# Attention probabilities of 43 steps and 16 tiles of a norm: transposed by DMA instead of by TensorE and the PSUM moves

## The chip, the cores and the metric

The kernel runs on the 8 cores of one Trainium2 chip. Each core works on one batch element of [2048, 1024] (the same program, other data); the cores don't speak to one another. The time is device microseconds (us) of the slowest core, from runs of the whole program. Engines are named as in the profile: PE is TensorE (matmuls and transposes), DVE VectorE, ACT ScalarE, POOL GpSimd, SP SyncE, which here only issues DMA.

## The reference, cut to what matters

Two layers. Layer 0 mixes tokens by dilated attention (three groups of heads with windows and dilations (128, 1), (512, 4), (2048, 16)) beside a convolution module; layer 1 by a short gated convolution. Every layer then adds and normalises, runs a SwiGLU FFN, normalises again and adds a gated embedding of p.

```python
# one head group; queries in blocks of 128, keys of the previous and of the own block
sc = jnp.einsum("brnqhe,brnkhe->brnhqk", qb, kk) * (e ** -0.5)
sc = jnp.where(mask[None, None, :, None], sc, NEG_INF)
m = jnp.max(sc, axis=-1, keepdims=True)
ex = jnp.exp(sc - m)
den = jnp.sum(ex, axis=-1)
o = jnp.einsum("brnhqk,brnkhe->brnqhe", ex, vv) / jnp.moveaxis(den, -1, -2)[..., None]
lse = m[..., 0] + jnp.log(den)
...
attn = sum over groups of softmax(lse over groups) * o
conv = silu(layer_norm(causal_depthwise_conv(a * sigmoid(gate), conv_w) + conv_b))
x = layer_norm(alpha * x + concat([attn, conv]) @ w_out)     # layer 0; layer 1: short_conv_mixer
x = layer_norm(alpha * x + swiglu(x))
x = x + (p[i] @ w_p) * sigmoid(x @ w_g)
```

## The kernel before, in words

Activations are held twice: as tokens (x_tok, 16 tiles of 128 tokens by 1024) and transposed (xT, 8 slabs of 128 channels by 2048 tokens), because every matmul contracts over partitions. Weights stream in by DMA on POOL's queue.

**Layer 0's mixer** works on 6 units (head group, pair of heads; UNITS). The even_order() list, written out by hand (L58 on), gives one order of events, and each engine walks the list and does its part of each event. In stage n (n = 0 to 5) unit n is projected, in 8 turns i: "qk" events with q/k matmuls (L559) and V matmuls (L586); VectorE applies the rotary embedding (L1191 to L1200), POOL adds the halves (rope_add, L1625). Between stages 0 and 1 lies the *gated stage*: 16 gated projections of the convolution module (L663), with attention steps 0 to 7 woven in. In stages 2 to 5 the attention of the unit projected before is woven in, step a = 8(n-1)+i at turn i, and stage 5 does unit 4 and unit 5, two steps in a pair of turns. An attention step (48 of them) handles two blocks of 128 queries of two heads:

- "s" scores(a): 8 matmuls (L602) into PSUM; VectorE masks (L1215) and takes the minimum (L1221) of the negated scores.
- "e" exponentials(a): ScalarE, four activations (L937) into Pb[a % 2].
- "t" transpose_p(a): PE transposes Pb in 4 to 8 tiles of 128x128 (L618) into PTB[0], a PSUM bank that it shares with "z", "cb" (conv_back, L697) and "mb" (merged_back, L648). The users of the bank follow one another in the order BANK0, and each waits until the one before it has been read (read0). p_move(a) copies the bank to PTt[a % 2], on ScalarE (L947) for the 32 steps of P_ON_ACT, on VectorE (L1233) for the other 16.
- "o" outputs(a): 4 to 8 matmuls of PTt with Vb (L636) into PTB[1]; ScalarE copies it to Ust (u_move, L968), and SP stores it to the scratch tensor scr (store_u, L1811).

"s" of a step comes at turn i, "e" at the start of the next turn, "t" in that turn behind the projections and "o" in the turn behind it (in the gated stage and in stage 5 further behind). Between "e" and "o" of one step lies about one turn in stages 2 to 4. In stages 2 to 4 "cb" and "cp" put the convolution's result back; in stages 4 and 5 the merge of the three groups runs ("ll" load_rows of scr into La, "ms", "mg", "mb"; L1827 to L1845, L987, L1280), with weights from statistics that go by scratch memory: ACT stores scs (L960), SP loads STL (load_statistics, L1815), VectorE computes them ("mw", L1245 to L1262).

**DMA queues.** SP, in the order of the list: scr stores, statistics, load_rows, x tiles (load_x), parameters, and in layer 1 and at both layers' ends DMA transposes of 128x1024 bf16 tiles (back1 L1870, back2 L1881, back3 L1888). POOL: load_unit(n+1) at the start of stage n (L1597, three times 512 KB), Wt, base, WmixE (L1679, 2 MB, stage 4, turn 2), later the FFN's ring pieces (L1588) and Wfo (L1693, 1 MB).

**Mixer output and the first norm of layer 0**: "out" mixer_out(t) for 16 tiles (L714), VectorE adds and normalises, ScalarE casts the tile to castt[t % 2]; norm_back(t) transposes it on PE (transpose_tile, L533) into PTB[1], three tiles behind, and ScalarE copies it to xT (L1097). The last tiles' events stand in ORDER[0], the FFN's list. FFN: L812 in, L838 out.

Of the kernel before, what the change touches and what calls it, by code (L numbers as in the profile page):

```python
# [6 lines left out]
BF16 = mybir.dt.bfloat16  # L7
# [5 lines left out]
NT = 16  # L13
# [6 lines left out]
K = 1024  # L20
# [19 lines left out]
WARM = 24  # L40
P_ON_ACT = [*range(8, 16), *range(24, 48)]

# [143 lines left out]
def build():  # L186
# [109 lines left out]
    dlt32 = sb("dlt32", [128, 8], F32, off_dg0)  # L296
    Pb = sb2("Pb", [128, 4, 256], BF16, off_dg0, 2 * K)
    sS = [sb("sS0", [128, 4, 256], F32, off_dg0 + 4 * K), sb("sS1", [128, 4, 256], F32, off_dg1 + 4 * K)]
# [26 lines left out]
    def half(i):  # L325
# [15 lines left out]

    pe_s, dve_ms, dve_mn, act_exp, pe_t, dve_pt, act_pt = (sem(n) for n in (
        "pe_s", "dve_ms", "dve_mn", "act_exp", "pe_t", "dve_pt", "act_pt"))
    pe_u, act_u = sem("pe_u"), sem("act_u")
# [16 lines left out]
    dve_xg1, dve_aff1 = sem("dve_xg1"), sem("dve_aff1")  # L361
    act_cast1, pe_tr1, act_xT1, d_x1 = sem("act_cast1"), sem("pe_tr1"), sem("act_xT1"), [sem("d_x1%d" % i) for i in range(2)]

# [121 lines left out]

    BANK0 = [u for u in EVEN if u[0] in ("t", "z", "cb", "mb")]
    BEFORE = dict(zip(BANK0[1:], BANK0))
# [42 lines left out]
    def tensor_program(pe):  # L530
# [77 lines left out]
        def transpose_p(a):  # L608
            if a == 0:
                pe.wait_ge(dve_const, 1)  # L610
# [4 lines left out]
            for bi, blk in enumerate(step_blocks(a)):  # L615
                for h in range(2):
                    for c in range(2 if qblock(UNITS[a // 8][1], blk)[0] else 1):
                        mm = pe.transpose(out=PTB[0][:, n * 128:(n + 1) * 128],  # L618
                                          in_=Pb[a % 2][:, 2 * bi + h, c * 128:(c + 1) * 128], identity=ident[:])
                        n += 1  # L620
            mm.then_inc(pe_t, 1)

# [44 lines left out]
        def phases_to_rows(c):  # L667
            if c == 0:
                pe.wait_ge(dve_glu, 16)
            pe.wait_ge(*read0(("z", c)))  # L670
# [46 lines left out]

        def norm_back(t):
            pe.wait_ge(act_cast1, t + 1)
            if t >= 1:  # L720
                pe.wait_ge(act_xT1, t)
            else:
                pe.wait_ge(act_u, 48)
            transpose_tile(castt[t % 2], 1, 8).then_inc(pe_tr1, 1)

        def even_mixer():
            for kind, v in EVEN:
                if kind == "qk":
                    project(*v)
                elif kind == "v7":  # L730
                    last_v()
                elif kind == "glu":
                    gated(v)
                elif kind == "s":
                    scores(v)
                elif kind == "t":
                    transpose_p(v)
                elif kind == "o":
                    outputs(v)
                elif kind == "z":  # L740
                    phases_to_rows(v)
                elif kind == "cv":
                    convolve(v)
                elif kind == "cb":
                    conv_back(v)
                elif kind == "mb":
                    merged_back(v)
                elif kind == "out":
                    mixer_out(v)
                elif kind == "nm" and v >= 3:  # L750
                    norm_back(v - 3)

# [16 lines left out]
        def layer_tail(l):  # L769
# [4 lines left out]
            for kind, a, b in ORDER[l]:  # L774
# [8 lines left out]
                if kind == "mo":  # L783
# [8 lines left out]
                    mm.then_inc(pe_mo, 1)  # L792
                elif kind == "tr1":
                    t = a
                    if l == 0:
                        norm_back(t)
# [99 lines left out]
        for i in range(WARM):  # L896
            pe.matmul(PD[2][:, 0:512], lhsT=Pb[1][:, 0, 0:128], rhs=Pb[1][:, 0:2, :].rearrange("p a b -> p (a b)"),
                      start=True, stop=True)
# [6 lines left out]
    def scalar_program(act):  # L905
# [22 lines left out]
        def exponentials(a):  # L928
            act.wait_ge(dve_mn, a + 1)
            if a >= 2:  # L930
                act.wait_ge(pe_t, a - 1)
            for i in range(4):
                bi, h = divmod(i, 2)
                blk = step_blocks(a)[bi]
                nk = 256 if qblock(UNITS[a // 8][1], blk)[0] else 128
                sblk = st_block(UNITS[a // 8][1], blk)
                act.activation(out=Pb[a % 2][:, i, 0:nk], in_=sS[a % 2][:, 2 * h + bi, 0:nk], func=AF.Exp, scale=-1.0,  # L937
                               bias=ST[:, a // 8, sblk, 2 + h:3 + h],
                               accum_out=ST[:, a // 8, sblk, h:h + 1]).then_inc(act_exp, 1)

        def p_move(a):
            if a not in P_ON_ACT:
                return
            n = 128 * sum(4 if qblock(UNITS[a // 8][1], b)[0] else 2 for b in step_blocks(a))
            act.wait_ge(pe_t, a + 1)
            act.wait_ge(pe_u, a - 1)
            act.activation(out=PTt[a % 2][:, 0:n], in_=PTB[0][:, 0:n], func=AF.Copy).then_inc(act_pt, 1)  # L947
# [74 lines left out]
        def even_mixer():  # L1022
# [6 lines left out]
            for kind, v in EVEN:  # L1029
# [19 lines left out]
                elif kind == "e":  # L1049
                    exponentials(v)  # L1050
                elif kind == "t":
                    p_move(v)
# [29 lines left out]
        def norm_slot(l, s):  # L1082
            t = s - 2
            if 0 <= t < NT:
                n = 16 * l + t
                act.wait_ge(dve_aff1, n + 1)
                if t >= 2 and l == 0:
                    act.wait_ge(pe_tr1, t - 1)
                elif t >= 2:
                    act.wait_ge(d_x1[t % 2], 16 * (t // 2))  # L1090
                act.activation(out=castt[t % 2][:], in_=x_tok[:, t, :], func=AF.Copy).then_inc(act_cast1, 1)
            if s < NT:
                squares(l, s)
            t = s - 3
# [91 lines left out]
    def vector_program(dve):  # L1186
# [16 lines left out]
        def masked(a):  # L1203
# [20 lines left out]
            d.then_inc(dve_mn, 1)  # L1224

        def p_move(a):
            if a in P_ON_ACT:
                return
            n = 128 * sum(4 if qblock(UNITS[a // 8][1], b)[0] else 2 for b in step_blocks(a))
            dve.wait_ge(pe_t, a + 1)  # L1230
            if a >= 2:
                dve.wait_ge(pe_u, a - 1)
            dve.tensor_copy(out=PTt[a % 2][:, 0:n], in_=PTB[0][:, 0:n]).then_inc(dve_pt, 1)  # L1233

# [104 lines left out]
        def even_mixer():  # L1339
# [6 lines left out]
            for kind, v in EVEN:  # L1346
# [26 lines left out]
                elif kind == "s":  # L1373
                    if v == 0:
                        dve.wait_ge(pool_const, 7)
                    masked(v)
                elif kind == "t":
                    p_move(v)
                elif kind == "z":
# [399 lines left out]
    def sync_program(sp):  # L1779
# [22 lines left out]
        def store_u(a):  # L1802
# [6 lines left out]
            for bi, blk in enumerate(step_blocks(a)):  # L1809
                hasp, st0, dil = qblock(g, blk)  # L1810
                sp.dma_start(out=scr[hp][st0:st0 + 127 * dil + 1:dil, PLACE[a // 8] - hp, :],  # L1811
                             in_=Ust[a % 3][:, bi, :]).then_inc(d_u[a % 3], 16)

        def load_statistics(hp):
            sp.wait_ge(d_ss, 32 * (hp + 1))  # L1815
# [48 lines left out]

        def back1(t):

            sp.wait_ge(act_cast1, 16 + t + 1)
            if t >= 2:
                sp.wait_ge(d_x1[t % 2], 16 * (t // 2))
            sp.dma_start(out=xT[:, :, t * 128:(t + 1) * 128], in_=castt[t % 2][:], transpose=True).then_inc(d_x1[t % 2], 16)  # L1870
# [40 lines left out]
        for l in range(2):  # L1911
# [125 lines left out]
```

## Time and profile before

| | us |
|---|---|
| median of 3 runs | 1874.15 (1873.45 to 1919.63) |
| the profiled execution | 1876.64 |
| its span, slowest core (core 2) | 1875.0 |
| spans of the 8 cores | 1864.8 to 1875.0 |
| granted clock of TensorE, mean over a core's span | 0.985 to 0.989 |
| gated stage / stage 1 / stage 2 / stage 3 | 85 to 147 / to 213 / to 273 / to 335 |
| stage 4 / stage 5 / mixer output | to 396 / to 475 / to 590 |

Times of the profile count from the span's start, on core 2. An idle time in brackets at the end of a row of a timeline is the wait of that engine before the instruction, with what ended it. A share of busy time is a mean over stages with different limits. Matmul rows of one line are put together ("x8"). The parts of a stage overlap at their edges, so its limits are rough.

### The profile page before, as it was taken

What the parts mean: (1) busy time and instruction counts of PE and PEld (TensorE: products, weight loads), DVE (VectorE), ACT (ScalarE), POOL (GpSimd) and SP (SyncE); (2) the same over time, 40 slices, a digit from 0 to 9 for tenths busy, and PEclk for the clock granted to TensorE, in tenths of its full rate; (3) what the DMA queues carried; (4) which work ended last, traced back from release to release, by engine and by line L of the source; (5) the groups of instructions that cost most, each with busy time, mean ns of one, the idle gap of its engine ahead of it and who ended that gap; (6) DMA issues with size and microseconds to landing.
All of it is one profiled execution on the core that took longest, in us unless ns stands there. A gap on an engine that the chain in (4) does not pass through costs nothing.

```text
span 1875.0 us, 27051 instructions; the slowest of 8 cores (1864.8 to 1875.0 us)
## 1 busy us (share of the span) xinstructions
PE 1768.8 (94%) x9307; PEld 890.3 (47%) x9488; DVE 1076.7 (57%) x1466; ACT 541.6 (29%) x1059; POOL 292.7 (16%) x304
## 2 busy tenths in 40 slices
PE   6998989988679999999999999999899999999998
PEld 2566656555334444444444444444344444444443
DVE  3455678677695424243486675667824334156668
ACT  2341246567575010101023331113510110101223
POOL 2315443322142000000011100002300000001011
PEclk7999999999799999999999999999999999999999
DMA  9633321735342622132112426113554312330224
GB/s 284 154 66 56 63 59 45 155 105 141 135 115 59 103 40 46 34 65 48 34 23 51 74 49 120 34 34 63 69 88 85 57 23 45 57 57 12 51 74 146
DMA packets 114452, 141.63 MB, mean 76 GB/s; under 512 B 77712, under 2 KB 89104, under 8 KB 111760
## 3 DMA queue, kind: packets, MB, share of 16 engines
q0 software_dynamic: 15120, 63.84, 20.0%
q1 hardware_dynamic: 97568, 74.88, 14.9%
q10 hardware_dynamic: 1632, 1.18, 0.3%
q8 instruction: 80, 1.31, 0.3%
q14 instruction: 52, 0.43, 0.1%
HBM read 168.97 MB, written 19.01 MB: 100 GB/s over the span
## 4 chain that ended last, share of the span: by engine, by line
PE 76%; DVE 9%; issue 5%; DMA 4%; ACT 3%; POOL 1%; SPq 0%; DVEq 0%; ACTq 0%; POOLq 0%
PE pd L812 32%; PE pd L838 16%; PE pd L765 9%; PE pd L856 6%; PE pd L559 4%; PE pd L663 3%; PE pd L586 2%; DVE x_tok L1468 2%; ACT Pb L937 1%; DVE x_tok L1409 1%; DMA xf<-xT 1%; DMA Wt<-conf_conv_we 1%; PE pd L868 1%; DMA xT<-castt 1%; PE pd L602 1%
## 5 line engine op out<-in xcount | busy, mean ns | idle before, releaser
L812 PE MATMUL pd<-xT,ring 128*128 128x512 bf16 x2507 | 553.3, 379 | 10.7 <-DVE hTf L1442 3.2
L812 PEld LDWEIGHTS pd<-xT,ring 128*128 128x128 bf16 x2560 | 249.7, 98 | 310.9 <-issue 11.9
L1071 ACT ACTIVATE sgt<-pd 128x512 f32<-128x512 f32 x176 | 104.9, 597 | 690.4 <-PE pd L812 690.2
L1442 DVE TENSOR_TENSOR hTf<-pd,sgt 128x512 bf16<-128x512 f32 x128 | 88.5, 692 | 345.8 <-ACT sgt L1071 345.8
L838 PE MATMUL pd<-Wfo,hTf 128*128 128x512 bf16 x1003 | 221.1, 379 | 1.1
L1457 DVE TENSOR_TENSOR x_tok<-x_tok,pd 128x1024 f32<-128x1024 f32 x128 | 156.4, 1222 | 57.2 <-PE pd L838 56.7
L559 PE MATMUL pd<-xT,ring 128*128 128x512 bf16 x543 | 175.0, 396 | 11.2 <-DVE xT L1330 5.1
L838 PEld LDWEIGHTS pd<-Wfo,hTf 128*128 128x128 bf16 x1024 | 100.2, 98 | 120.8
L765 PE MATMUL pd<-xT,ring 128*128 128x512 bf16 x502 | 114.8, 383 | 3.7 <-DVE yT L1505 2.6
L856 PE MATMUL pd<-Wpg,x2T 128*128 128x512 bf16 x502 | 115.2, 379 | 0.7 <-DVE sigt L1483 0.2
L1588 POOL DMA_DIRECT2D ring<-ffn_w_in x40 | 21.4, 536 | 603.4 <-PE pd L812 523.7
L1196 DVE TENSOR_TENSOR rt<-pd,rope 128x512 f32<-128x512 f32 x96 | 66.1, 689 | 78.7 <-PE pd L559 32.2
L937 ACT ACTIVATE Pb<-sS,ST 128x256 bf16<-128x256 f32 (+1 forms) x192 | 86.1, 452 | 63.5 <-DVE ST L1221 63.5
L586 PE MATMUL pd<-ring,xT 128*128 128x256 bf16 x384 | 89.0, 277 | 5.3 <-DVE ring L1337 3.4
L559 PEld LDWEIGHTS pd<-xT,ring 128*128 128x128 bf16 x576 | 55.6, 101 | 76.8 <-issue 31.4
L586 PE MATMUL pd<-wx,xT 128*128 128x256 bf16 x384 | 89.1, 273 | 0.9 <-issue 0.2
L1442 DVE TENSOR_TENSOR hTq<-pd,sgt 128x512 bf16<-128x512 f32 x48 | 33.2, 691 | 92.2 <-ACT sgt L1071 92.1
L1625 POOL TENSOR_TENSOR qb<-rt,rt 128x1024 bf16<-128x1024 f32 x24 | 56.6, 2358 | 176.7 <-DVE rt L1200 170.3
L838 PE MATMUL pd<-Wfo,hTq 128*128 128x512 bf16 x376 | 83.8, 379 | 0.4
L765 PEld LDWEIGHTS pd<-xT,ring 128*128 128x128 bf16 x512 | 50.3, 99 | 64.9 <-issue 5.7
L856 PEld LDWEIGHTS pd<-Wpg,x2T 128*128 128x128 bf16 x512 | 49.9, 98 | 61.3 <-issue 2.0
L1625 POOL TENSOR_TENSOR kb<-rt,rt 128x1024 bf16<-128x1024 f32 x24 | 56.6, 2357 | 124.4 <-DVE rt L1200 124.4
(160 smaller groups left out, 2253.7 us busy)
## 6 DMA issues: line engine op xcount, KB each, us to landing
ring<-ffn_w_in POOLq DMA_DIRECT2D x40, 512.0 KB, 5.2
scr<-Ust SPq DMA_DIRECT2D x80, 128.0 KB, 2.0
Wfo<-ffn_w_out POOLq DMA_DIRECT2D x10, 1024.0 KB, 10.4
x_tok<-x SPq DMA_DIRECT2D x16, 512.0 KB, 5.4
out<-x_tok SPq DMA_DIRECT2D x15, 512.0 KB, 2.9
xf<-xT SPq DMA_DIRECT2D x3, 2048.0 KB, 21.9
ring<-even_w_in POOLq DMA_DIRECT2D x9, 512.0 KB, 8.6
La<-scr SPq DMA_DIRECT2D x11, 384.0 KB, 3.4
```

The costliest lines, as they stand in the source:

```text
L559: qk = pe.matmul(half(h % 3), lhsT=wqk[:, d, part * 128:(part + 1) * 128], rhs=xT[:, d, tc * 512:(tc + 1) * 512], start=(d == 0), stop=(d ...
L586: return pe.matmul(half(3)[:, j * 256:(j + 1) * 256], lhsT=xT[:, d, st0:st0 + 127 * dil + 1:dil], rhs=wqkv[3 * (n % 2) + 2][:, d, :], star ...
L765: mm = pe.matmul(bank, lhsT=src[:, d, j2 * 128:(j2 + 1) * 128], rhs=xT[:, d, tc * 512:(tc + 1) * 512], start=(d == 0), stop=(d == 7))
L812: mm = pe.matmul(bank[:, w * 512:(w + 1) * 512], lhsT=w_in[:, d, w * 128:(w + 1) * 128], rhs=xT[:, d, tc * 512:(tc + 1) * 512], start=(d = ...
L838: mm = pe.matmul(bank[:, hf * 512:(hf + 1) * 512], lhsT=ht, rhs=wo[:, hf * 512:(hf + 1) * 512], start=(ff == 0), stop=(ff == nf - 1))
L856: mm = pe.matmul(bank[:, hf * 512:(hf + 1) * 512], lhsT=x2T[t % 2][:, c, :], rhs=Wpg[:, c, hf * 512:(hf + 1) * 512], start=(c == 0), stop= ...
L937: act.activation(out=Pb[a % 2][:, i, 0:nk], in_=sS[a % 2][:, 2 * h + bi, 0:nk], func=AF.Exp, scale=-1.0, bias=ST[:, a // 8, sblk, 2 + h:3 ...
L1071: act.activation(out=sgt[n % 2][:], in_=PD[PAIR[l]["in", f, tc]][:, 0:512], func=AF.Silu).then_inc(act_silu, 1)
L1196: dve.tensor_tensor(out=rt1[:, part, :], in0=bank, in1=rcs[:, 0, cs], op=ALU.mult)
L1442: dve.tensor_tensor(out=ht, in0=PD[PAIR[l]["in", f, tc]][:, 512:1024], in1=sgt[n % 2][:], op=ALU.mult).then_inc(dve_h, 1)
L1457: dve.tensor_tensor(out=xt, in0=xt, in1=bank[:], op=ALU.add).then_inc(dve_acc, 1)
L1625: pool.tensor_tensor(out=(qb, kb)[i % 2][n % 2][:, :, tc * 512:(tc + 1) * 512], in0=rt1[:], in1=rt2[:], op=ALU.add).then_inc(pool_rope, 1)
```

## The change

For steps 0 to 42 the probabilities are transposed by a DMA on SP's queue, p_back(a), from Pb[a % 2] (now laid out as one row of 1024 columns) straight to PTt[a % 2]; steps 43 to 47 keep the transposes on PE, with the move on ScalarE. SP issues p_back(a) at the event "e" of step a for a < 33, and right behind store_u(a-2) for 33 to 42. outputs(a) waits for the landing (d_pt); exponentials(a) waits until the transposition of step a-2 has landed. VectorE's p_move is gone, and PTB[0]'s chain of users has only the last five of the "t" in it. In layer 0's first norm the 16 tiles are transposed by DMA on SP (back1(0, t), at "nm" of tile t+2, the last two in ORDER[0]) in place of norm_back and ScalarE's copy; castt(t) and the FFN's first pieces wait for d_x1.

```diff
+P_ON_PE = 43
...
-    BANK0 = [u for u in EVEN if u[0] in ("t", "z", "cb", "mb")]
+    BANK0 = [u for u in EVEN if u[0] in ("z", "cb", "mb") or u[0] == "t" and u[1] >= P_ON_PE]
...
     def moved(a):
-        return (act_pt, sum(b in P_ON_ACT for b in range(a + 1))) if a in P_ON_ACT else (
-            dve_pt, sum(b not in P_ON_ACT for b in range(a + 1)))
+        return (act_pt, a - P_ON_PE + 1) if a >= P_ON_PE else (d_pt[a % 2], 16 * (a // 2 + 1))
+
+    def columns(a):
+        return 128 * sum(4 if qblock(UNITS[a // 8][1], b)[0] else 2 for b in step_blocks(a))
...
         def transpose_p(a):
             pe.wait_ge(act_exp, 4 * a + 4)
-            if a >= 1:
-                pe.wait_ge(*read0(("t", a)))
-            n = 0
...
+            pe.wait_ge(*read0(("t", a)))
+            transpose_tile(Pb[a % 2], 0, columns(a) // 128).then_inc(pe_t, 1)
...
-        def norm_back(t):
-            pe.wait_ge(act_cast1, t + 1)
...
-            transpose_tile(castt[t % 2], 1, 8).then_inc(pe_tr1, 1)
...
-                elif kind == "t":
+                elif kind == "t" and v >= P_ON_PE:
                     transpose_p(v)
...
                     f, tc = a, b
-                    if f < 3 and l == 0:
-                        pe.wait_ge(act_xT1, 4 * tc + 4)
-                    elif f < 3:
+                    if f < 3:
                         for i in range(2):
-                            pe.wait_ge(d_x1[i], 16 * (2 * tc + 2))
+                            pe.wait_ge(d_x1[i], 16 * (8 * l + 2 * tc + 2))
...
         def exponentials(a):
             act.wait_ge(dve_mn, a + 1)
             if a >= 2:
-                act.wait_ge(pe_t, a - 1)
+                act.wait_ge(*((pe_t, a - 1 - P_ON_PE) if a - 2 >= P_ON_PE else moved(a - 2)))
...
-                if t >= 2 and l == 0:
-                    act.wait_ge(pe_tr1, t - 1)
-                elif t >= 2:
-                    act.wait_ge(d_x1[t % 2], 16 * (t // 2))
+                if t >= 2:
+                    act.wait_ge(d_x1[t % 2], 16 * (8 * l + t // 2))
...
-            if l == 0 and 0 <= t < NT:
-                act.wait_ge(pe_tr1, t + 1)
-                act.activation(out=xT[:, :, t * 128:(t + 1) * 128], in_=PTB[1][:].rearrange("p (c n) -> p c n", c=8),
-                               func=AF.Copy).then_inc(act_xT1, 1)
...
-        def p_move(a):
-            if a in P_ON_ACT:
-                return
...
-            dve.tensor_copy(out=PTt[a % 2][:, 0:n], in_=PTB[0][:, 0:n]).then_inc(dve_pt, 1)
...
+        def p_back(a):
+            sp.wait_ge(act_exp, 4 * a + 4)
+            if a >= 2:
+                sp.wait_ge(pe_u, a - 1)
+                sp.wait_ge(d_pt[a % 2], 16 * (a // 2))
+            n = columns(a)
+            sp.dma_start(out=PTt[a % 2][:, 0:n].rearrange("p (c n) -> p c n", n=128), in_=Pb[a % 2][:, 0:n],
+                         transpose=True).then_inc(d_pt[a % 2], 16)
...
         for kind, v in EVEN:
-            if kind == "o":
+            if kind == "e" and v < 33:
+                p_back(v)
+            elif kind == "o":
                 store_u(v)
+                if 33 <= v + 2 < P_ON_PE:
+                    p_back(v + 2)
...
+            elif kind == "nm" and v >= 2:
+                back1(0, v - 2)
...
-                if kind == "tr1" and l == 1:
-                    back1(a)
+                if kind == "tr1" and (l == 1 or a >= 14):
+                    back1(l, a)
```

## Rows read from the trace of the kernel before

**Rows 1.** The chain that ended last, by engine (section 4 of the page).

```profile
PE 76%; DVE 9%; issue 5%; DMA 4%; ACT 3%; POOL 1%; SPq 0%; DVEq 0%; ACTq 0%; POOLq 0%
```

**Rows 2.** Groups by line: busy us, mean ns | idle before them, releasers.

```profile
L618 PE MATMUL ptb<-ident,Pb 128*128 128x128 bf16 x300 | 25.4, 224 | 10.4 <-ACT attnT L996 5.5 <-ACT Pb L937 4.7
...
L533 PE MATMUL ptb<-ident,castt 128*128 128x128 bf16 x160 | 12.6, 223 | 12.8 <-ACT xT L1097 11.8 <-ACT Uk L968 0.9
```

**Rows 3.** Timeline of PE, gated stage: start us, us, engine, line, operation.

```profile
101.58 0.61 PE L618 MATMUL ptb<-ident,Pb 128*128 128x128 bf16 x8
102.12 0.61 PE L602 MATMUL pd<-kb,qb 64*128 64x256 bf16 x8
```

**Rows 4.** Timeline of PE, stage 3.

```profile
287.29 0.39 PE L618 MATMUL ptb<-ident,Pb 128*128 128x128 bf16 x4
287.61 1.08 PE L602 MATMUL pd<-kb,qb 64*128 64x256 bf16 x8
288.98 0.61 PE L697 MATMUL ptb<-ident,Zn 128*128 128x128 bf16 x8 [0.28 <-DVE PTt L1233]
```

**Rows 5.** Timeline of DVE, stages 2 and 4, line L1200.

```profile
227.69 0.68 DVE L1200 SCALAR_TENSOR_TENSOR rt<-pd,rope 128x512 f32<-128x512 f32 x1
...
235.62 0.68 DVE L1200 SCALAR_TENSOR_TENSOR rt<-pd,rope 128x512 f32<-128x512 f32 x1
...
366.18 0.68 DVE L1200 SCALAR_TENSOR_TENSOR rt<-pd,rope 128x512 f32<-128x512 f32 x1
...
373.22 0.68 DVE L1200 SCALAR_TENSOR_TENSOR rt<-pd,rope 128x512 f32<-128x512 f32 x1
```

**Rows 6.** The line L1870, back1 of layer 1, over the whole span.

```profile
  PE pd L812: 2.0, 1
...
DMA to landing us min/median/max: 3.0/3.1/17.9
```

**Rows 7.** DMA issues, windows 269:285, 355:373, 1349:1367, whole span: KB each, us to landing.

```profile
ring<-even_w_in POOLq DMA_DIRECT2D x3, 512.0 KB, 11.4
...
WmixE<-even_w_out POOLq DMA_DIRECT2D x1, 2048.0 KB, 17.7
scr<-Ust SPq DMA_DIRECT2D x6, 128.0 KB, 10.6
...
Wfo<-ffn_w_out POOLq DMA_DIRECT2D x1, 1024.0 KB, 17.5
...
xT<-castt SPq DMA_TRANSPOSE x2, 16.8
...
scr<-Ust SPq DMA_DIRECT2D x80, 128.0 KB, 2.0
Wfo<-ffn_w_out POOLq DMA_DIRECT2D x10, 1024.0 KB, 10.4
```

**Rows 8.** Timelines of POOL, PE and ACT around the three steps.

```profile
268.94 1.72 POOL L1597 DMA_DIRECT2D ring<-even_w_in  x3
...
276.56 0.39 PE L636 MATMUL ptb<-Vb,PTt 128*128 128x128 bf16 x4
...
330.69 1.07 POOL L1597 DMA_DIRECT2D wx<-even_w_in  x2
...
355.24 0.57 POOL L1679 DMA_DIRECT2D WmixE<-even_w_out  x1
...
338.42 0.61 PE L636 MATMUL ptb<-Vb,PTt 128*128 128x128 bf16 x8
...
355.79 0.19 ACT L937 ACTIVATION_READ_ACCUMULATOR Pb<-sS,ST 128x1 f32 x1
...
359.83 0.33 PE L636 MATMUL ptb<-Vb,PTt 128*128 128x128 bf16 x3
```

**Rows 9.** Window 480 to 490 (busy us, PEclk, DMA); PE's timeline before it.

```profile
480.00:490.00 10.00, 5.88 (x28) 2.91 (x26) 7.10 (x17) 6.15 (x20) 0.00 (x0) 0.50 0.25 92
...
477.26 1.03 PE L602 MATMUL pd<-kb,qb 64*128 64x256 bf16 x8 [4.45 <-POOL kb L1625]
```

More of the change, by code:

```diff
@@ L40 @@
 WARM = 24
-P_ON_ACT = [*range(8, 16), *range(24, 48)]
+P_ON_PE = 43
 def qblock(g, blk):
@@ L340, in build @@
     pe_glu, act_glu, dve_glu = sem("pe_glu"), sem("act_glu"), sem("dve_glu")
-    pe_s, dve_ms, dve_mn, act_exp, pe_t, dve_pt, act_pt = (sem(n) for n in (
-        "pe_s", "dve_ms", "dve_mn", "act_exp", "pe_t", "dve_pt", "act_pt"))
+    pe_s, dve_ms, dve_mn, act_exp, pe_t, act_pt = (sem(n) for n in ("pe_s", "dve_ms", "dve_mn", "act_exp", "pe_t", "act_pt"))
+    d_pt = [sem("d_pt%d" % i) for i in range(2)]
     pe_u, act_u = sem("pe_u"), sem("act_u")
@@ L361, in build @@
     dve_xg1, dve_aff1 = sem("dve_xg1"), sem("dve_aff1")
-    act_cast1, pe_tr1, act_xT1, d_x1 = sem("act_cast1"), sem("pe_tr1"), sem("act_xT1"), [sem("d_x1%d" % i) for i in range(2)]
+    act_cast1, d_x1 = sem("act_cast1"), [sem("d_x1%d" % i) for i in range(2)]
     d_wfo = [sem("d_wfo%d" % i) for i in range(2)]
@@ L608, in transpose_p @@
         def transpose_p(a):
-            if a == 0:
-                pe.wait_ge(dve_const, 1)
             pe.wait_ge(act_exp, 4 * a + 4)
-            if a >= 1:
-                pe.wait_ge(*read0(("t", a)))
-            n = 0
[L615 to L621, printed above, removed]
+            pe.wait_ge(*read0(("t", a)))
+            transpose_tile(Pb[a % 2], 0, columns(a) // 128).then_inc(pe_t, 1)
         def outputs(a):
@@ L668, in phases_to_rows @@
             if c == 0:
+                pe.wait_ge(dve_const, 1)
                 pe.wait_ge(dve_glu, 16)
-            pe.wait_ge(*read0(("z", c)))
+            else:
+                pe.wait_ge(*read0(("z", c)))
             for i in range(8):
@@ L749, in even_mixer @@
                     mixer_out(v)
-                elif kind == "nm" and v >= 3:
-                    norm_back(v - 3)
         def odd_third(w, n, j, tc, bank):
@@ L896, in tensor_program @@
         for i in range(WARM):
[L897 removed]
+            pe.matmul(PD[2][:, 0:512], lhsT=Pb[1][:, 0:128], rhs=Pb[1][:, 0:512],
                       start=True, stop=True)
@@ L936, in exponentials @@
                 sblk = st_block(UNITS[a // 8][1], blk)
-                act.activation(out=Pb[a % 2][:, i, 0:nk], in_=sS[a % 2][:, 2 * h + bi, 0:nk], func=AF.Exp, scale=-1.0,
+                act.activation(out=Pb[a % 2][:, n:n + nk], in_=sS[a % 2][:, 2 * h + bi, 0:nk], func=AF.Exp, scale=-1.0,
                                bias=ST[:, a // 8, sblk, 2 + h:3 + h],
                                accum_out=ST[:, a // 8, sblk, h:h + 1]).then_inc(act_exp, 1)
+                n += nk
         def p_move(a):
-            if a not in P_ON_ACT:
-                return
-            n = 128 * sum(4 if qblock(UNITS[a // 8][1], b)[0] else 2 for b in step_blocks(a))
-            act.wait_ge(pe_t, a + 1)
+            n = columns(a)
+            act.wait_ge(pe_t, a - P_ON_PE + 1)
             act.wait_ge(pe_u, a - 1)
@@ L1050, in even_mixer @@
                     exponentials(v)
-                elif kind == "t":
+                elif kind == "t" and v >= P_ON_PE:
                     p_move(v)
@@ L1224, in masked @@
             d.then_inc(dve_mn, 1)
-        def p_move(a):
-            if a in P_ON_ACT:
[L1228 to L1232, printed above, removed]
-            dve.tensor_copy(out=PTt[a % 2][:, 0:n], in_=PTB[0][:, 0:n]).then_inc(dve_pt, 1)
         def merge_weights(batch):
@@ L1376, in even_mixer @@
                     masked(v)
-                elif kind == "t":
-                    p_move(v)
                 elif kind == "z":
@@ L1863, in load_x, with back1 @@
             sp.dma_start(out=x_tok[:, t, :], in_=x_d[t * 128:(t + 1) * 128, :]).then_inc(d_x[t % 8], 16)
[L1865 to L1869, printed above, removed]
+        def back1(l, t):
+            sp.wait_ge(act_cast1, 16 * l + t + 1)
+            if l or t >= 2:
+                sp.wait_ge(d_x1[t % 2], 16 * (8 * l + t // 2))
             sp.dma_start(out=xT[:, :, t * 128:(t + 1) * 128], in_=castt[t % 2][:], transpose=True).then_inc(d_x1[t % 2], 16)
```

13 lines of the change are left out of this document (3 added, 10 removed).

## Prediction

> **What bounds the kernel now.** I read the page's chain first. TensorE (PE) carries 76% of the chain that ended last; VectorE (DVE) 9% [rows 1]. So a saving on PE can be worth its own length, but only in the stretches where PE sets the pace, and each stretch has to be asked. The groups by line give the size of what is moved: 300 transposes of probabilities keep PE 25.4 us, 160 of the helper line L533 12.6 us, of which 128 are the norm's [rows 2]. Such busy time overlaps that of the neighbours, so it is no saving yet. PE's own timeline gives the time that a transposition *holds* PE: eight probability transposes at 101.58 are followed by the scores at 102.12, so .54 us [rows 3]; four (a pair of blocks with 128 keys each) from 287.29 to 287.61, .31 to .32 us, and the next user of the PSUM bank, the convolution's conv_back (L697), waits .28 us for the move out of it [rows 4]. VectorE's timeline says which loop is PE's: its rotary operation L1200 comes every 7.93 us in stage 2, where GpSimd's and VectorE's rotary chain is the slow one, and every 7.04 us in stage 4, a loop of merge work on ScalarE (ACT) and VectorE [rows 5]. In the gated turns PE has no gap; in stage 3 next to none.
>
> The profiled execution took 1876.64 us; the median shown is 1874.15, so 2.5 less. The sum is made on 1876.64 and 2.5 is taken off.
>
> **Part 1: 43 steps' transposes leave PE.** *Gated stage* (steps 0 to 5): PE without a gap, one transposition a turn [rows 3]: .4 for the first, which has six tiles, 5 x .54, and 2 x .54 for steps 6 and 7 just behind it: -4.2. *Stage 2* (steps 8 to 14): its 7.93 us turn belongs to VectorE and GpSimd [rows 5], so nothing. *Stage 3* (16 to 23): PE-bound; two short transpositions x .31, five long x .54 [rows 3, 4], and seven waits of conv_back like the one of .28, from .23 to .64, 2.1 together: 5.4 less. *Stage 4* (24 to 31): the loop of ACT and VectorE [rows 5]: nothing. *Stage 5* (32 to 42): a loop of VectorE and ACT too; ACT's p_move lies in the chain of waits at two places (of some 1.2 us), of which I take 1.5 in all; 0 to 4. Elsewhere VectorE's and ACT's p_moves stand beside PE's projections, which hide them, and are not counted; were they not hidden, VectorE's .7 a turn would be a further gain in stage 2.
>
> **What replaces them.** Each is one DMA transpose on SyncE's queue (SP). The trace has the same operation in layer 1: 16 of them, landing after 3.0 to 17.9 us, median 3.1 [rows 6]. What they have is the time from the last exponential to the outputs that read them: step 26's exponentials end at 355.79+.19 and its outputs start at 359.83, so 3.9 us, the tightest; step 15, ending at 270.4, has 6.2, step 23, at 333.5, 4.9 [rows 8]. At 3.1 us none would be late; what counts is how long they take beside the big loads, and the two ends lie far apart. Lower end: 3.1 us, no cost. Upper end: two transposes issued beside Wfo's load of 1 MB landed after 16.8 us, and the load itself took 17.5 against a median of 10.4 [rows 7]. I take the middle reading: a transfer issued behind a GpSimd load lands when the load has ended, since the scr stores, 2.0 us at the median of 80, took 10.6 at the median of six beside WmixE's 2 MB of 17.7 us [rows 7]. Then a transposition lands 3.1 us after the load.
>
> Queue by queue: behind a p_back on SP stand store_u, the loads of statistics and rows and the next p_back. They wait for exponentials that are done by their turn in the order list, and a short issue stands against a turn of 7 to 8 us; GpSimd's queue is not touched. exponentials(a) now waits for the landing of a-2, two turns earlier (some 14 us): hidden unless a landing takes over 10 us.
>
> **Three places where a load stands in the way.**
> - Step 15: exponentials end 270.4, the three ring loads of unit 4 were issued from 268.94 and take 11.4 us, the last until about 281; landing about 284 against an output at 276.56 [rows 7, 8]: +7.4.
> - Step 23: three loads issued from 330.1, two of them as in [rows 8], end about 342.6, landing about 345.7 against 338.42: 7.3 late. PE's next units and the statistics for the merge (scs store, load, merge weights) follow, which also waited for this load before, so VectorE's rotary of turn 26 moves only from 352.1 to about 357: +4.9 (1.5 to 7.3).
> - Step 26: exponentials end 356.0; WmixE (2 MB) was issued at 355.24 and takes 17.7 us [rows 7], so until 372.9; landing 376.0 against 359.8 [rows 8]: 16.2 late. In this turn PE is ready some 2.5 us before VectorE's rotary pair, whose second half is at 366.18 [rows 5]: +13.7 (0 to 23).
>
> The loads of units 1 to 3 (issued about 75, 102 and 208) meet steps with two turns of cover, or end before the output is due; a step beside them costs nothing, 3 at most together. Bounds of the three together: 0 (all landings of 3.1) and 44 (R2).
>
> **Clock.** In 480 to 490 the granted clock was 0.50, the lower of the two levels (1.2 GHz), and PE had stood idle for 4.45 us just before [rows 9]. Each of the three stalls above is longer than that. After it eight score matmuls took 1.03 us in place of .61 [rows 3, 9], for some 3 us of matmuls, so 1.5 us more for each stall: +4.5 (0 to 9).
>
> **Part 2: the norm's 16 tiles.** A tile's transposes hold PE .45 us, with a wait for ACT's move (11.8 us over 16 [rows 2]). But the mixer's output stage is VectorE's until about 562, where both are near full. Only its last third counts: seven tiles x .45 and some 2 us of the waits, -5 (0 to -7). Against it, transposes 14 and 15 leave SP beside the first Wfo load (1 MB, issued 580.7), as in layer 1, where two took 16.8 [rows 7] and PE waited 2.0 in all [rows 6]: +2 (0 to 9, if nothing else can be computed before them). So -3.
>
> **Sum.** -4.2 (gated) -5.4 (stage 3) +7.4 (step 15) +4.9 +13.7 +4.5 -1.5 -3 = +16.4, so 1893.0 on the profiled scale and **1890.5 us** on that of the median. A measurement of this kernel can tell about 2% (37 us) from no change; I forecast no change by that bound, on the slow side.
>
> The Trainium skill has a rule against the change: "VectorE: DVE Perf Modes", The three transpose paths, advises TensorE for a 128x128 transpose whose destination may be PSUM and puts a DMA transpose at 1309 ns and TensorE's at 390. By it eight tiles would cost 10.5 us by DMA and 3.1 on PE. The trace agrees with neither: eight together hold PE .54 us, and eight land after 3.1.
>
> **Rivals.**
> - *R1, transposes pass the loads* (chance .22). They land in 3.1 us, PE's whole saving stays: -4.2 -5.4 -1.5 -3 = -14.1, and stage 3's earlier start lets the .7 and .6 us waits and part of stage 4's slack go, -2: 1860.5 profiled, **1858**. For it: the median landing of 3.1 in a stretch with DMA busy by half. Against: the stores beside loads, 10 to 16 us [rows 7]. It decides if step 26's transposition lands before about 362. The Trainium skill speaks for it: "DMA: Bandwidth & Descriptors", Queues, rings and completion order, has each engine go round robin between queues packet by packet, so that a small transfer would not wait for the end of a large one. The trace's stores beside WmixE, 10.6 against 2.0, do not agree.
> - *R2, both slow each other* (chance .22). Wfo took 17.5 instead of 10.4 beside two transposes, 1.7 times [rows 6, 7]. If the late loads stretch so, each of the three delays does: (7.4+4.9+13.7) x .7 = +18.2: 1911 profiled, **1909**, slower than before by 35 us. Place: stages 3 to 4; it decides from a WmixE landing above 25 us. Against: only 17 of 1875 us show such a pair.
> - *R3, hidden both ways* (.10): half of the delays are taken up by VectorE's loops of stages 3 and 4, so 13.5 in place of 30.5 (delays 26.0, clock 4.5), with the same gains of 14.1: 1876.0 profiled, **1873.5**, no change. For it: 2.5 us of slack at step 26 may stand in every turn of stage 4; against: a stall once made is not won back there.
>
> **Numbers.** Forecast .44, R1 .22, R2 .22, R3 .10, other .02. The range of the forecast alone is 1881 to 1901 (step 26 from 9.7 to 20, clock from 0 to 9, in the profile 1884 to 1904). For 8 in 10 I take 1857 to 1911, R1 and R2 at the ends. Faster by over 2% (below 1836.7) needs a gain of 37 us, more than all PE transposes together with their waits: .02. Slower by over 2% (above 1911.6) needs R2's upper half: .11. Within: .87.
>
> **What would show it.** Right: L636 waits for DMA PTt at steps 15, 23 and 26 of about 7, 7 and 14 us, and elsewhere none; L1200 turns of stage 3 shorter by .5 us; a clock below 1.0 behind the stalls; the gated stage's turns at 8.0. Wrong: a landing near 3 us beside WmixE (R1); WmixE above 25 us or turns longer in stages 2 and 5, where DMA stores run (R2); waits of exponentials for PTt's landing, which I put at nothing.

## The result, and the profile after

The changed kernel takes 1895.1 us at the median of its runs, the kernel before 1874.15; the ratio is 1.0108 with a 95% interval of 1.0093 to 1.0123, so 17 to 23 us slower; by the bound of 2% that is no change, on the slow side. The forecast was 1890.5 us. Some executions of each kernel run slower, at a lower granted clock; the ratios here and below leave them out and the medians don't, which moves a median by up to .5 us. The profiled execution's span is 1893.5 us on its slowest core (core 1), 18.5 more than before. The lines have moved: outputs is L630 (L636 before), the scores L606 (L602), the exponentials L918 (L937), the rotary operation L1173 (L1200), p_back L1783, WmixE's load L1641.

The page of the changed kernel, busy time and chain, beside [rows 1]:

```profile
PE 1773.5 (94%) x9100; PEld 870.2 (46%) x9100; DVE 1067.3 (56%) x1450; ACT 511.8 (27%) x1016; POOL 292.8 (15%) x304
...
PE 75%; DVE 9%; DMA 6%; issue 4%; ACT 3%; POOL 1%; SPq 1%; DVEq 0%; ACTq 0%; POOLq 0%
```

VectorE and ScalarE are relieved by 9 and 30 us against the busy times of the page before, 1076.7 and 541.6. PE's busy time hasn't fallen (1768.8 before, with some matmul records missing): some of its matmuls ran at the lower clock. The chain has a DMA share of 6%, before 4%. What PE waited for says which DMA (engine, tile and line, what it waited for: us in total, times, longest):

```profile
PE ptb L630 <- DMA PTt<-Pb: 40.6, 10, 11.1
PE pd L710 <- ACT attnT L976: 11.3, 5, 3.7
```

PE's timeline has the ten waits. These are the long ones; the first is of step 2, the next three are steps 15, 23 and 26, the last is in stage 5. The last bracket is the wait ahead of the instruction:

```profile
118.42 0.61 PE L630 MATMUL ptb<-Vb,PTt 128*128 128x128 bf16 x8 [2.67 <-DMA PTt<-Pb]
...
283.17 0.59 PE L630 MATMUL ptb<-Vb,PTt 128*128 128x128 bf16 x4 [10.05 <-DMA PTt<-Pb]
...
347.81 1.01 PE L630 MATMUL ptb<-Vb,PTt 128*128 128x128 bf16 x8 [6.56 <-DMA PTt<-Pb]
...
380.88 0.58 PE L630 MATMUL ptb<-Vb,PTt 128*128 128x128 bf16 x4 [11.07 <-DMA PTt<-Pb]
...
457.44 1.01 PE L630 MATMUL ptb<-Vb,PTt 128*128 128x128 bf16 x8 [3.65 <-DMA PTt<-Pb]
```

And this is how long the transposes took: the line p_back over the whole span, then its issues for steps 15, 23 and 26 alone; then the second and third of the three loads beside step 15, last WmixE's load, issued .9 us ahead of step 26's transposition:

```profile
L1783 SPq DMA_TRANSPOSE PTt<-Pb x43: 1174/1228/6114, 87.1 to 478.7; - x43
...
DMA to landing us min/median/max: 2.4/3.1/15.1
...
L1783 SPq DMA_TRANSPOSE PTt<-Pb x1: 2661/2661/2661, 269.8 to 269.8; - x1
DMA to landing us min/median/max: 13.0/13.0/13.0
...
L1783 SPq DMA_TRANSPOSE PTt<-Pb x1: 1422/1422/1422, 336.9 to 336.9; - x1
DMA to landing us min/median/max: 10.6/10.6/10.6
...
L1783 SPq DMA_TRANSPOSE PTt<-Pb x1: 1797/1797/1797, 365.4 to 365.4; - x1
DMA to landing us min/median/max: 15.1/15.1/15.1
...
L1559 POOL DMA_DIRECT2D ring<-even_w_in x2: 547/552/557, 269.5 to 270.0; - x2
DMA to landing us min/median/max: 10.3/11.4/12.5
...
L1641 POOL DMA_DIRECT2D WmixE<-even_w_out x1: 573/573/573, 364.5 to 364.5; - x1
DMA to landing us min/median/max: 15.6/15.6/15.6
```

The median of 3.1 is that of [rows 6]; it belongs to steps of eight tiles. Steps of four tiles, such as 15 and 26, land in 2.4 us when no load is under way. Step 26's transposition landed at 365.4 + 15.1 = 380.5, WmixE at 364.5 + 15.6 = 380.1: the small transfer came home .4 us behind the large one. Step 15's landed at 269.8 + 13.0 = 282.8, .3 us behind the third load (270.0 + 12.5 = 282.5), although that load was issued .2 us after it. It was the same at step 2: its transposition was issued at 103.1, the last load .7 us later, and the transposition landed .8 us behind that load. So a load need not be issued ahead of a transposition to hold it.

Where the time went is best read from one operation that each turn has, VectorE's L1200 (L1173 after), counted from the last one of stage 0 so that the cores' different starts fall out. The table is worked out from the timelines of the slowest cores: how much later (+) or earlier (-) than in the kernel before a turn comes, in us. The last three columns are experiments 2, 4 and 10.

| turn | after | probabilities alone | spread loads | steps chosen, norm on PE |
|---|---|---|---|---|
| first of stage 1 | +3.0 | -1.2 | -1.3 | -1.3 |
| first of stage 2 | -0.6 | -3.6 | -5.0 | -3.4 |
| first of stage 3 | -1.1 | -4.1 | -5.5 | -4.0 |
| next (behind step 15) | +7.6 | +4.1 | -6.4 | -5.2 |
| first of stage 4 | +2.5 | -1.0 | -11.5 | -10.9 |
| third of stage 4 (behind step 23) | +8.6 | +5.1 | -13.9 | -13.2 |
| fifth of stage 4 (behind step 26) | +19.9 | +15.8 | -13.2 | -11.9 |
| first of stage 5 | +20.5 | +16.5 | -12.4 | -10.8 |
| last of stage 5 | +21.7 | +14.8 | -12.0 | -12.2 |

In the first column three jumps, +8.7, +6.1 and +11.3, stand on a slow gain in stage 3 (from +7.6 to +2.5 in seven turns). The jumps and this gain are much the same as a mean over the eight cores (+8.2, +5.9, +10.0; -5.1). Single differences of 1 or 2 us are not so firm: in experiments 3 and 6, which work the gated stage as the kernel before does, the slowest core enters stage 1 at +1.7. Behind each jump TensorE's granted clock was lower, the third number from the end in these windows (the last row is an undisturbed one of stage 3; columns as in [rows 9]):

```profile
283.00:289.00 6.00, 5.83 (x36) 3.69 (x37) 1.17 (x2) 1.18 (x2) 0.00 (x0) 0.70 0.19 56
347.00:353.00 6.00, 5.19 (x28) 3.24 (x28) 0.20 (x1) 0.60 (x1) 0.00 (x0) 0.63 0.50 55
381.00:387.00 6.00, 6.00 (x28) 3.23 (x28) 2.05 (x6) 1.41 (x4) 0.00 (x0) 0.62 0.53 165
310.00:330.00 20.00, 20.00 (x158) 14.00 (x157) 17.18 (x19) 15.44 (x35) 7.13 (x3) 1.00 0.28 71
```

With levels of 1.2 and 2.4 GHz, .62 to .70 is a mixture of the two, in the 6 us behind a wait of 6 to 11 us.

### The profile page after: what moved, and what is told of

The parts are those of the page before. It is cut to its first block, busy times and chain, and to the rows that moved or that the text cites. A ratio compares the mean times of both kernels' runs of the same rounds, so it can differ in the third digit from the quotient of the medians.

```text
span 1893.5 us, 26407 instructions; the slowest of 8 cores (1871.4 to 1893.5 us)
## 1 busy us (share of the span) xinstructions
PE 1773.5 (94%) x9100; PEld 870.2 (46%) x9100; DVE 1067.3 (56%) x1450; ACT 511.8 (27%) x1016; POOL 292.8 (15%) x304
## 3 DMA queue, kind: packets, MB, share of 16 engines
q0 software_dynamic: 15120, 63.84, 20.5%
## 4 chain that ended last, share of the span: by engine, by line
PE 75%; DVE 9%; DMA 6%; issue 4%; ACT 3%; POOL 1%; SPq 1%; DVEq 0%; ACTq 0%; POOLq 0%
PE pd L792 32%; PE pd L818 16%; PE pd L751 9%; PE pd L836 5%; DMA PTt<-Pb 4%; PE pd L563 4%; PE pd L657 2%; PE pd L590 2%; DVE x_tok L1430 2%; DVE x_tok L1371 2%; ACT Pb L918 1%; PE pd L848 1%; DMA xf<-xT 1%; DMA Wt<-conf_conv_we 1%; DVE sS L1188 1%
## 5 line engine op out<-in xcount | busy, mean ns | idle before, releaser
L792 PE MATMUL pd<-xT,ring 128*128 128x512 bf16 x2560 | 558.4, 380 | 5.7 <-DVE hTf L1404 3.2
L563 PE MATMUL pd<-xT,ring 128*128 128x512 bf16 x576 | 185.5, 398 | 12.0 <-ACT xT L905 8.4
L751 PE MATMUL pd<-xT,ring 128*128 128x512 bf16 x512 | 115.6, 383 | 3.4 <-DVE yT L1467 2.6
L918 ACT ACTIVATE Pb<-sS,ST 128x256 bf16<-128x256 f32 (+1 forms) x192 | 86.1, 452 | 74.3 <-DVE ST L1194 67.5
```

Source lines behind the costliest of these rows:

```text
L563: qk = pe.matmul(half(h % 3), lhsT=wqk[:, d, part * 128:(part + 1) * 128], rhs=xT[:, d, tc * 512:(tc + 1) * 512], start=(d == 0), stop=(d ...
L751: mm = pe.matmul(bank, lhsT=src[:, d, j2 * 128:(j2 + 1) * 128], rhs=xT[:, d, tc * 512:(tc + 1) * 512], start=(d == 0), stop=(d == 7))
L792: mm = pe.matmul(bank[:, w * 512:(w + 1) * 512], lhsT=w_in[:, d, w * 128:(w + 1) * 128], rhs=xT[:, d, tc * 512:(tc + 1) * 512], start=(d = ...
L918: act.activation(out=Pb[a % 2][:, n:n + nk], in_=sS[a % 2][:, 2 * h + bi, 0:nk], func=AF.Exp, scale=-1.0, bias=ST[:, a // 8, sblk, 2 + h:3 ...
```

## The experiments

The theory to test: the whole loss is a few transposes that a load of GpSimd's queue holds back until it has ended. Against it: transposes by DMA cost time wherever they run.

**1. The colliding steps back on PE.**

```diff
-P_ON_PE = 43
+P_ON_PE = [15, 23, 26, 27, 28, *range(43, 48)]
```

> The changed kernel with steps 15, 23, 26, 27 and 28 back on PE (transposes on PE, move on ScalarE), the ones whose DMA transposes were issued beside a load of GpSimd's queue and landed 7.7 to 15.1 us later. Theory H (the whole loss is these landings, held back by the load): the waits of L630 of 10.05, 6.56 and 11.07 us go, and with them the half-clock matmuls behind them; what is left is the gain of stage 3 (about -5), the late transposes of stage 5 (+3) and the norm (-4): 1868 to 1874 us, ratio 0.997 to 1.000. Rival G (transposes cost time wherever they run, by their packets or by the clock): only a part comes back, 1884 or more, ratio above 1.005.

Measured: ratio 0.9986 (0.9952 to 1.002), median 1871.23. Five steps of 43 bring back the whole loss of 20 us, within the interval. The theory stands, and the rival, at 1.005 or more, falls. What is left of waits for transposes is 17.9 us, of which 4.66 at step 24, which I had left by DMA beside the same load of unit 5 as step 23.

**2. The probabilities alone by DMA** (the norm as before; the norm's part of the diff taken back).

> The changed kernel with the norm's 16 tiles back on PE (norm_back and ScalarE's copy), only the probabilities by DMA. My forecast had the norm's part at -3 us; the traces show +22.4 before it and +18.5 at the end, so -4. Theory: 1897 to 1900 us, ratio 1.012 to 1.014. Rival (the norm's part costs time, its transposes beside Wfo landed after up to 13.9 us): ratio below 1.010.

Measured: ratio 1.009 (1.0056 to 1.0124), from two executions, which can't be told from 1.0108. The expectation of 1.012 to 1.014 is not borne out; in the trace the stage behind the last turn of stage 5 took as long as before (+14.8 there, +14.9 at the end), while in the changed kernel it took 3.8 less (+21.7, +17.9).

**3. The norm alone by DMA** (the kernel before with the norm's part of the diff).

> The kernel before with only the norm's 16 tiles by DMA. Theory: -3 to -4 us, 1870 to 1871, ratio 0.998. Rival (the norm's part costs or gives nothing by itself): 1874 or more, ratio 1.000 or above.

Measured: ratio 0.9983 (0.9934 to 1.0032): inconclusive. But the trace has the wait that I had put at +2, for the transposes of tiles 14 and 15, at the FFN's start:

```profile
600.15 20.04 PE L796 MATMUL pd<-xT,ring 128*128 128x512 bf16 x79 [3.50 <-DMA xT<-castt]
```

**4. Loads spread out, all 43 steps and the norm by DMA.** A piece is of 256 KB.

```diff
-                load_unit(n + 1)
             for i in range(8):
+                if n < 5 and i < 6:
+                    load_third(n + 1, i // 2, i % 2)
...
-                    pool.dma_start(out=WmixE[:], in_=ewout_d).then_inc(d_wmix, 16)
+                if n == 4 and i >= 2 or n == 5 and i < 2:
+                    f = 8 * (n - 4) + i - 2
+                    pool.dma_start(out=WmixE[:, f, :], in_=ewout_d[:, f, :]).then_inc(d_wmix, 16)
```

> The changed kernel with the loads spread out: units 2 to 5 in six pieces of 256 KB, one before each of the first six rope_adds of a stage, and WmixE in eight of 256 KB, one a turn from turn 2 of stage 4; nothing else moved. Theory H (a transposition lands when the load ahead of it has ended): each lands after at most 3.1 + 2 us, the three waits of 10.05, 6.56 and 11.07 go, and stage 3's gain stays: 1866 to 1872 us, ratio 0.996 to 0.999. Rival F (a transposition beside any load is slow for another reason, its own small packets taking turns with the load's): more of them land late now, 2 to 5 us in each turn, and the time stays above 1885, ratio above 1.006.

Measured: ratio 0.9972 (0.9954 to 0.999). The same transposes in the same places, and only the loads cut: all of the loss goes, 26 us lie between this kernel and the changed one. The waits are there still, but short, 18.0 us in 11, the longest 3.4. Theory H had each land after at most 5.1 us; in the three turns of stage 4 that have two pieces each they took 6.5, 5.5 and 6.1, where 2.4 is usual without a load (here the median of nine in stage 4, beside the pieces):

```profile
WmixE<-even_w_out POOLq DMA_DIRECT2D x7, 256.0 KB, 4.6
wx<-even_w_in POOLq DMA_DIRECT2D x3, 256.0 KB, 6.3
PTt<-Pb SPq DMA_TRANSPOSE x9, 4.7
```

**5. A longer load ahead of step 26.** Experiments 1 and 4 say that the loads do it, not how. If the transposition is held until the load has ended, then twice the load doubles its landing; if its delay goes by its own size alone, it lands at the same time as before.

```diff
                     pool.dma_start(out=WmixE[:], in_=ewout_d).then_inc(d_wmix, 16)
+                    pool.dma_start(out=spare, in_=ewout_d).then_inc(d_spare, 16)
```

> The changed kernel with a second transfer of 2 MB (the same weights, into a spare DRAM tensor that nothing reads) right behind WmixE on GpSimd's queue. In the changed kernel step 26's transposition (4 tiles, the small kind) was issued .9 us behind WmixE and landed after 15.1 us, .4 us after WmixE's own 15.6. Theory H (held until everything ahead on that queue has ended): it lands some 10 to 15 us later, at 25 to 31 us, L630's wait grows from 11.07 to about 22 to 26, and the time grows by 10 to 15 us. Rival T (its packets take turns with those of the load one by one, so its delay goes by its own packets): it lands after about 15 as before, and the time stays within 3 us of the changed kernel's.

Measured, one run: 1904.96 us, 10 more than the changed kernel, and the trace says the rest. Here are, by line, the two loads and step 26's transposition; from PE's timeline the outputs that waited for it; and from SP's timeline the next transposition:

```profile
L1643 POOL DMA_DIRECT2D WmixE<-even_w_out x1: 572/572/572, 359.6 to 359.6; - x1
DMA to landing us min/median/max: 18.6/18.6/18.6
...
L1644 POOL DMA_DIRECT2D spare<-even_w_out x1: 521/521/521, 360.1 to 360.1; - x1
DMA to landing us min/median/max: 32.2/32.2/32.2
...
L1787 SPq DMA_TRANSPOSE PTt<-Pb x1: 1649/1649/1649, 360.5 to 360.5; - x1
DMA to landing us min/median/max: 32.1/32.1/32.1
```

```profile
392.99 0.58 PE L632 MATMUL ptb<-Vb,PTt 128*128 128x128 bf16 x4 [28.09 <-DMA PTt<-Pb]
```

```profile
367.54 21.26 SPq L1787 DMA_TRANSPOSE PTt<-Pb  x1
```

The transposition landed at 360.5 + 32.1 = 392.6, the second load at 392.3. So the delay grows with the load, as the theory has it, and the rival's 15 us is out. The wait of 28.09 is beyond the 22 to 26 that I had expected.

That the packets take turns is not excluded by this, though the rival was put so. It took the transposition for the smaller transfer, and in packets it is the larger one. Here are the packets of the two queues in three windows: GpSimd's queue in the changed kernel, 364 to 381 (WmixE alone); SP's queue there, 231.7 to 235.9 (a transposition of four tiles and two scr stores); SP's queue in the kernel before, 308 to 315 (two scr stores alone):

```profile
q0 software_dynamic: 144, 2.10, 70.7%
...
q1 hardware_dynamic: 832, 0.39, 33.5%
...
q1 hardware_dynamic: 288, 0.26, 11.0%
```

A transposition of four tiles is thus 832 - 288 = 544 packets, 2 MB of load are 144 and the 4 MB of this run 224. If they took turns one by one, the loads would be through first, and the transposition would land just behind them, as it did. A transfer with fewer packets than the loads beside it is the statistics' store of the kernel before, on ScalarE's queue: 144 packets beside the 432 of the three loads at the start of stage 3. It was issued .4 us behind the last of them and landed at 270.5 + 11.0 = 281.5, the loads at 283.4 (the second and third load, then the store):

```profile
L1597 POOL DMA_DIRECT2D ring<-even_w_in x2: 547/552/558, 269.6 to 270.1; - x2
DMA to landing us min/median/max: 11.4/12.4/13.3
...
L960 ACTq DMA_DIRECT2D scs<-ST x1: 336/336/336, 270.5 to 270.5; - x1
DMA to landing us min/median/max: 11.0/11.0/11.0
```

So the store was not held until all that was ahead had ended; nor did it take even turns, by which a third of the packets would have been through in about a third of the loads' 14.5 us, some 5 us (an estimate from these rows). The Trainium skill ("DMA: Bandwidth & Descriptors", Queues, rings and completion order) has each engine go round robin between its queues, packet by packet; with the packets counted as here, the landings of the transposes don't contradict it, and that of the store does not fit it well. No run has varied the number of packets, so what holds the transposition stays open.

**6. Control: spread loads in the kernel before.**

> Control: the kernel before (all transposes on PE) with the loads spread out as in the run with spread loads. If spreading helps only by letting the transposes through, this is the kernel before: ratio 0.998 to 1.001. If the spread loads help by themselves (the statistics' store and load before the merge weights and the La loads pass too: up to 5 us at turn 2 of stage 4), ratio about 0.996 and the DMA transposes are worth no more than some 4 us.

Measured: ratio 0.9998 (0.9987 to 1.0009). Spreading gives nothing by itself; it is worth 26 us only to a kernel that has small transfers with a deadline.

**7. Pieces behind the turn's transposition.**

```diff
+                a = 8 * (n - 1) + i - 1
+                if 2 <= n < 5 and i >= 1 and a not in P_ON_PE:
+                    pool.wait_ge(*moved(a))
+                if n < 5 and (n == 1 and i < 6 or n > 1 and 1 <= i < 7):
...
+                    load_third(n + 1, j // 2, j % 2)
```

> As the run with spread loads, but in stages 2 to 4 each piece is issued behind the turn's rope_add and once the transposition of that turn has landed. Theory H: the transposes of stages 2 to 4 land in about 3 us instead of 3.7 to 6.5; the waits left in stage 4 (1.92, 1.02) and stage 2 (1.45, 2.11) go, 2 to 4 us better than with spread loads alone: ratio 0.993 to 0.996. Rival: the waits left come from SyncE's own queue (scr stores and La loads ahead of the transposition), and nothing changes: ratio 0.997.

Measured: ratio 0.9984 (0.9973 to 0.9994), no better than experiment 4. I had thought that a piece sent after one landing would be home before the next transposition. In stage 4 it isn't so: the first piece of a turn waits for the landing on GpSimd, and goes out .2 us before the next transposition, which then is late, which sends the next piece late (GpSimd's and SP's timeline, and that transposition's landing):

```profile
348.66 0.57 POOL L1570 DMA_DIRECT2D wx<-even_w_in  x1 [0.69 <-DMA PTt<-Pb]
```

```profile
348.83 1.20 SPq L1806 DMA_TRANSPOSE PTt<-Pb  x1
```

```profile
L1806 SPq DMA_TRANSPOSE PTt<-Pb x1: 1195/1195/1195, 348.8 to 348.8; - x1
DMA to landing us min/median/max: 6.9/6.9/6.9
```

So the first theory failed on the place of the wait, which brought piece and transposition together instead of keeping them apart. It is the pieces, and not SP's own queue as the rival had it, that make the landings long: in and around stage 2 of this trace the transposes of four tiles with a piece issued .9 us ahead took 3.8 to 4.2 us, and those without one 2.4 us, with the same neighbours on SP.

**8. The same, steps 32 to 42 on PE.**

> The same with steps 32 to 42 back on PE. Stage 5 lost 2 to 3 us in the changed kernel and in the run with spread loads (waits of 3.39, 1.88, 2.62 for transposes issued behind store_u). Theory: they come from the place in SyncE's queue, so 2 us better than without it, ratio 0.992 to 0.995. Rival: stage 5's loop belongs to VectorE and ScalarE and ScalarE's moves come back in it: no better, or 1 to 2 us worse.

Measured: ratio 0.9962 (0.9948 to 0.9976), median 1865.88. Its interval touches that of experiment 7, whose trace lost 2 us in stage 5 (-11.4 in its second turn, -9.2 in its last but one) where this one stays at -7.8: the direction is as expected, the size not shown. As a mean over the eight cores stage 5 took .7 us less than in the kernel before, in experiment 7 .3 us more.

**9 to 11. Choice of steps.** In the table, stages 2, 4 and 5 give no gain with DMA transposes. So: by DMA only where PE sets the pace. The first line of the diff is that of 9 and 10, with the loads spread out; the second that of 11, with the loads and the norm of the kernel before.

```diff
-P_ON_PE = 43
+P_ON_PE = [*range(8, 15), *range(26, 48)]
+P_ON_PE = [3, *range(8, 16), *range(23, 48)]
```

> Spread loads, and DMA transposes only where PE sets the pace: steps 0 to 7 and 15 to 25 by DMA, steps 8 to 14 and 26 to 47 on PE, the norm by DMA. Theory S (the gain lives in the gated stage and in stage 3 alone): up to stage 4 as with spread loads (-12 to -13 us), and nothing given back in stages 4 and 5, where that run lost 2: ratio 0.994 to 0.996. Rival: ScalarE's moves and the PSUM bank's chain in stages 4 and 5 cost what the DMA transposes saved there, ratio 0.997.

> The same with the norm's 16 tiles on PE. My forecast had the norm's part at -3; the single runs left it open (norm alone 0.9983 with an interval of half a per cent either way, probabilities alone 1.009 against 1.0108 for both). Theory: 2 to 4 us more than with the norm by DMA. Rival (a wash: what PE saves it waits for transposes held beside Wfo's load): within 1 us of it.

> Nothing but the choice of steps: loads as in the kernel before, norm on PE, DMA for steps 0, 1, 2, 4 to 7 and 16 to 22 (PE-bound stages, and not beside a load), all else on PE. Theory: gated stage -3 or so, stage 3 about -5 to -6, no stall: 5 to 9 us under the kernel before, ratio 0.995 to 0.997. Rival (stage 1's Wt loads and the statistics' way through scratch memory before stage 4 take the gain back): ratio 0.999 or above.

Measured: 9: 0.9965 (0.9953 to 0.9978), median 1865.63. 10: 0.9958 (0.9945 to 0.9971), median 1864.72, the fastest of all. 11: 0.998 (0.9967 to 0.9993), median 1868.37. With 19 steps of 48 by DMA the whole gain is there; without touching a load about half of it (and there I had chosen wrongly in the gated stage: the transposition that unit 2's load holds is step 2's, which I had left by DMA, and not step 3's; the trace has stage 1 at +0.6). Between 9 and 10 lies .9 us by the medians (1.3 by the ratios, whose intervals overlap), so for the norm's part the rival holds: a wash. Theory S of run 9, that nothing is given back in stages 4 and 5, is not borne out: its trace goes from -13.9 at the third turn of stage 4 to -10.8 at the end of stage 5, that of experiment 4 from -13.9 to -12.0. I read it so that the moves on ScalarE cost there what the transposes cost, which is not shown by itself; the ratios of 4, 8, 9 and 10 overlap.

## Why the prediction was right, step by step

The three places, and the rule that a transposition beside a load comes home with the load, were as forecast. Several sizes were off; that they made up for one another, so that the total came out within 5 us, is luck.

- *The landing*: forecast was a transposition of 3.1 us behind the end of the load. At steps 2, 15, 23 and 26 and in experiment 5 it landed .3 to .9 us behind the last load. The 3.1 that the sum added at each place was too much.
- *Step 15*: forecast +7.4, clock apart (1.5). Measured +8.7 with it, PE's wait 10.05. Right; shown by experiments 1 and 4. The landing, about 284 in the forecast and 282.8 in the trace, came near by two errors: 3.1 too much, and the last of the three loads ended in the kernel before at 283.4, not at about 281 (11.4 was the median of the three).
- *Step 23*: forecast +4.9 and 1.5. Measured +6.1, wait 6.56. Right.
- *Step 26*: forecast +13.7 and 1.5; measured +11.3, wait 11.07. WmixE took 15.6 us in place of the 17.7 of [rows 7], and the landing came .4 us behind it. That term of the sum was too large by 4.
- *Stage 3*: forecast -5.4; behind step 15 the changed kernel gained 5.1 (+7.6 to +2.5), experiment 4 gained 6.0 over the whole stage. Right; its turns were shorter by .7 us, not .5. *Stage 2*: nothing, as forecast: the table's second and third lines differ by .5. *Stage 4* without its stalls: nothing, too (+19.9 to +20.5).
- *Gated stage*: forecast -4.2, and "a step beside them costs nothing, 3 at most together" for the loads of units 1 to 3. The "nothing" failed. Unit 2's load, from 102.8, held the transposition issued at 103.1 for 15.0 us; PE stood 2.67 us for it (118.42 above), with a granted clock of .72 in the 6 us behind. I had weighed the cover by its turns and not in us: from 103.1 to the output's due time at 115.8 lie 12.7 us, and the loads needed 15. The slowest core entered stage 1 at +3.0 and stage 2 at -0.6, but it is an outlier: the mean over the eight cores is -1.7 and -2.7, and in experiments 1, 2 and 5, where step 2 is held in the same way (landings of 12 to 14 us), it is -2.1 to -2.8 and then -3.7 to -4.3. Without that collision (experiments 4 and 10) the mean is -3.0 and then -3.8. So the gain of some 4 us was real, and came in part only in stage 1; the collision cost about 1 us, and more on this one core.
- *Stage 5*: forecast -1.5; measured +1.2 on the slowest core, +.1 as a mean over the cores, and in experiments 2 and 5, with the same transposes there, 0 and -.3. So no gain. ScalarE's moves went, but three outputs waited 2.6, 3.7 and 2.1 us for transposes that stand on SP behind store_u and took 5.1 to 5.9 us beside its stores and row loads. The exponentials, whose wait for a landing I had put at nothing, waited 6.9 us in three turns, all of them here.
- *Clock*: forecast 4.5 for three stalls. It is in the jumps above; PEclk .62 to .70 over 6 us each says that it is there, but its own share was not measured apart.
- *Norm*: forecast -3. The changed kernel has -3.8 between the last turn of stage 5 and the end, but the single traces of the other kernels with the norm by DMA have -3.5 to +2.2 (experiments 1, 3 to 5, 7 to 9), those with it on PE -1.8 to +.5 (2, 6, 10, 11). The forecast wait for tiles 14 and 15 is absent on the changed kernel's slowest core; on five of the other cores it is 1.7 to 5.3 us. Right by the one trace only; the runs of 9 and 10 say a wash.
- *R1* (transposes pass the loads) is out by all of the landings of 10.6 to 15.1 and by experiment 5. Its argument, that a small transfer passes a large one, failed in the word small: 544 packets stood beside 144. *R2* (both slow each other, WmixE above 25 us) is out, WmixE took 15.6. *R3* is out: the jumps came to 26.1 us with the clock, where it had 13.5 (its own words, half of the delays, would give 15 to 17.5).

The sum was +16.4; the changed kernel's trace shows +17.9 at the end (the mean over its cores +15.4), the ratio +20.2.

## What to carry to other kernels

A DMA with a deadline came home here only when the loads beside it did, loads on another queue and issued up to .7 us after it included. Small in bytes did not mean small: look at the packets too. List the loads with issue time and length, the transfers with a deadline with issue time and due time in us, and look for overlaps before moving work from an engine to DMA. Cutting and spreading the loads, which was worth nothing by itself, then turned a loss of 20 us into a gain of 5; choosing the steps did it too, with a gain of 4. And move work only in stages whose pace the relieved engine sets: 19 steps of 48 gave all that there was here.

## What the runs showed of the hardware that was not expected

- A transposition of four tiles issued .9 us behind a 2 MB load landed .4 us after it, and with 4 MB ahead .3 us after that: 15.1 and 32.1 us in place of 2.4.
- Loads issued .2 us (step 15) and .7 us (step 2) after a transposition held it too.
- The issue itself is held. While step 26's transposition was under way with 4 MB ahead, the next one's instruction on SyncE took 21.26 us (1.2 at the median), until 388.8; nothing behind it on that queue could go out before. The scr stores issued between the two, at 362.3, landed after 30.6 us.
- With two pieces of 256 KB under way a transposition of four tiles took 6.9 us, nearly three times its 2.4.
